# Hybrid RG-LRU and attention block on eight cores: VectorE copies the next line's first gate sums out of PSUM while ScalarE takes its square roots

## The reference, cut to what matters

```python
def rglru_coeffs(xc, wa, ba, wx, bx, lam):
    r = jax.nn.sigmoid(jnp.einsum('blnd,nde->blne', xb, wa) + ba)   # recurrence gate
    i = jax.nn.sigmoid(jnp.einsum('blnd,nde->blne', xb, wx) + bx)   # input gate
    log_a = -LRU_C * r * jax.nn.softplus(-lam)
    a = jnp.exp(log_a)
    coef = jnp.sqrt(-jnp.expm1(2.0 * log_a))                        # sqrt(1 - a*a)
    return a, coef * (i * xf)
# then h[t] = a[t] * h[t-1] + b[t] per channel, forward and backward, both added,
# times gelu(gate branch), then the output projection
```

## Time and profile before

| what | value |
| --- | --- |
| median of 3 timed runs (lowest, highest) | 3960.41 us (3803.53, 4261.93) |
| the profiled execution's own time | 3797.51 us |
| its span, first to last instruction, slowest core (core 2) | 3795.9 us |
| spans of the 8 cores | 3766.0 to 3795.9 us |
| mean granted TensorE clock of the cores | 0.957 to 0.962 of full speed |

### The profile page before, as it was taken

How to read it: one execution, slowest core, us unless ns; L and a number is a source line. 1 busy time by engine, 2 the same in 40 slices (tenths; PEclk the granted TensorE clock), 3 DMA queues, 4 the chain that set the end, 5 groups by cost and what they waited for, 6 DMA issues and landing times.

```text
span 3795.9 us, 51533 instructions; the slowest of 8 cores (3766.0 to 3795.9 us)
## 1 busy us (share of the span) xinstructions
PE 3480.0 (92%) x15292; PEld 1460.8 (38%) x15292; DVE 2856.2 (75%) x3064; ACT 2195.1 (58%) x2549; POOL 710.0 (19%) x621
## 2 busy tenths in 40 slices
PE   5787898899899789899999999999999999999989
PEld 2333343333333223334434434434434444444434
DVE  1687786566677788898798798798798798788732
ACT  2566668677688666565465465465465465556410
POOL 2466650000000000220120120130040040040030
PEclk8899999988989799999999999999999999999999
DMA  8555657977767642322632532543543443452454
GB/s 198 150 151 154 179 165 160 205 172 169 201 157 183 169 148 71 91 89 88 164 114 88 161 115 88 154 121 92 139 134 94 126 147 93 117 161 84 119 172 139
DMA packets 282622, 523.93 MB, mean 138 GB/s; under 512 B 29968, under 2 KB 139024, under 8 KB 281104
## 3 DMA queue, kind: packets, MB, share of 16 engines
q1 hardware_dynamic: 239712, 427.82, 38.3%
q0 software_dynamic: 19312, 57.03, 9.0%
q10 hardware_dynamic: 23328, 35.79, 2.7%
HBM read 470.19 MB, written 114.56 MB: 154 GB/s over the span
## 4 chain that ended last, share of the span: by engine, by line
PE 71%; ACT 7%; DVE 7%; issue 6%; DMA 5%; SPq 2%; POOL 1%; ACTq 0%; DVEq 0%; POOLq 0%
PE psq L468 71%; SPq L452 2%; DVE acc L474 2%; ACT tmp L459 1%; DVE xt L474 1%; ACT pt L459 1%; ACT L459 1%; DMA rb<-RD 1%; DVE tq L482 1%; DMA Q<-qo 1%; ACT ab L459 1%; DMA wm<-w_mod 1%; DVE xo L482 1%; DMA x<-XC 1%; DMA wmd<-w_mod 1%
## 5 line engine op out<-in xcount | busy, mean ns | idle before, releaser
L459 ACT ACTIVATE pt<-psq 128x1024 bf16<-128x1024 f32 x1088 | 1103.0, 1022 | 881.8 <-PE psq L468 824.8
L474 DVE TENSOR_TENSOR acc<-acc,pt 128x1024 f32<-128x1024 f32 x960 | 1230.0, 1281 | 231.2 <-ACT pt L459 192.8
L468 PE MATMUL psq<-mt,wr 128*128 128x512 bf16 x3328 | 819.2, 380 | 16.7 <-ACT mt L459 8.4
L468 PE MATMUL psq<-pt,Vt 128*128 128x512 bf16 x2176 | 655.7, 380 | 41.1 <-ACT pt L459 40.7
L468 PE MATMUL psq<-qh,KT 128*128 128x512 bf16 x2176 | 651.6, 380 | 0.0
L468 PEld LDWEIGHTS psq<-mt,wr 128*128 128x128 bf16 x3328 | 321.4, 98 | 432.9 <-issue 66.4
L468 PE MATMUL psq<-hL,wt 128*128 128x512 bf16 x1664 | 413.8, 401 | 21.3 <-ACT to L459 13.4
L468 PE MATMUL psq<-aT,wr 128*128 128x512 bf16 x1408 | 333.4, 379 | 0.3 <-DVE den L474 0.3
L452 POOL DMA_DIRECT2D RD<-rec x8 | 4.3, 538 | 1721.1 <-DVE rec L486 1721.1
L468 PEld LDWEIGHTS psq<-pt,Vt 128*128 128x128 bf16 x2176 | 197.1, 97 | 332.5 <-issue 135.3
L468 PE MATMUL psq<-xc,gw 128*128 128x512 bf16 (+1 forms) x832 | 276.0, 421 | 44.9 <-ACT ab L459 39.6
(11 more groups left out here) (128 smaller groups left out, 3860.1 us busy)
## 6 DMA issues: line engine op xcount, KB each, us to landing
wr<-WFI SPq DMA_DIRECT2D x176, 512.0 KB, 3.6
wr<-WFO SPq DMA_DIRECT2D x128, 352.0 KB, 3.1
x<-XC SPq DMA_DIRECT2D x70, 512.0 KB, 8.6
xc<-XCB SPq DMA_DIRECT2D x126, 256.0 KB, 6.6
wr<-WOL SPq DMA_DIRECT2D x64, 320.0 KB, 4.7
XC<-xo SPq DMA_DIRECT2D x80, 228.0 KB, 3.2
xt<-xT SPq DMA_DIRECT2D x8, 2048.0 KB, 12.1
wmd<-w_mod SPq DMA_DIRECT2D x16, 1024.0 KB, 6.1
```

The costliest lines, as they stand in the source:

```text
L459: return S.add("act", lambda e: e.activation(out=out, in_=in_, func=func, **kw), reads, writes, dur=0.17 + 0.000833 * fsz(out) + 0.09 * na ...
L468: return S.add("pe", lambda e: e.matmul(out, lhsT=lhsT, rhs=rhs, start=start, stop=stop), reads, writes, dur=d, lat=0.3)
L474: return S.add(eng, lambda e: e.tensor_tensor(out=out, in0=in0, in1=in1, op=op), reads, writes, dur=edur(eng, fsz(out), 1.13e-3))
```

## The change

Three things change, all in the loop over the steps.

1. At the end of a line (`idx == 4`), after the gates of step `k + 2` (the next line's first chunk of 1024), `step_copy(k + 2)` has VectorE copy both gate sums from PSUM into the `ab` and `wb` buffers that the chunk will use. The loads and the gates of step `k + 3` are emitted right behind, ahead of `window(li)`. At `idx == 0` the tanh of that chunk then reads and writes these SBUF buffers, and `gate_mm` isn't emitted again. This happens at 19 of the 20 line ends.
2. The square of the chunk at `idx == 2` moves from VectorE to ScalarE, in all 20 lines. It is emitted at `idx == 4`.
3. The planner's estimate for a VectorE copy of 1024 columns becomes 1.23 us (it was 0.82).

```diff
-                     dur=0.1 + fsz(out) * (1.1e-3 if eng == "pool" else 0.7e-3))
+                     dur=0.1 + fsz(out) * (1.1e-3 if eng == "pool" or fsz(out) == 1024 else 0.7e-3))
...
+    def step_a(k, copied=False):
...
+        if copied:
+            ab, wb = aslots[(li, c)], wslots[(li, c)]
+            sa, sx, ra, rx = ab.t[:, 0:n], wb.t[:, 0:n], [ab.r], [wb.r]
+        else:
+            ab, wb = step_slots(k)
+            sa, sx = ps2[0][:, 0:n], ps2[1][:, 0:n]
...
+    def step_copy(k):
+        ab, wb = step_slots(k)
+        cast("dve", ab.t[:, :], ps2[0][:, :], [ps[0].r, ps[1].r], [ab.r])
+        cast("dve", wb.t[:, :], ps2[1][:, :], [ps[2].r, ps[3].r], [wb.r])
...
-        if idx in (2, 3):
+        if idx == 2:
             square(k - 1, "dve")
...
             square(k - 4, "act")
+            square(k - 2, "act")
             square(k - 1, "act")
             square(k, "act")
...
             g_evict()
+            if k + 2 < nst:
+                step_copy(k + 2)
+                step_load(k + 3)
+                gate_mm(k + 3)
             window(li)
             gw_load(li + 2)
         else:
-            step_a(k + 1)
-            if k + 2 < nst:
+            step_a(k + 1, idx == 0 and k > 0)
+            if k + 2 < nst and (idx > 0 or k == 0):
                 gate_mm(k + 2)
```

More of the change, by code:

```diff
@@ L990, in flush_ev, with step_slots @@
             evq.pop(0)()
-    def step_a(k):
+    def step_slots(k):
         li, m, d, c = steps[k]
-        c0, n = chunks[c]
-        ci = d * 10 + m
         ab = acR.next() if c == 0 else aR.next()
@@ L999, in step_a @@
         wslots[(li, c)] = wb
-        nb = (n + 511) // 512
-        ra = [ps[h].r for h in range(nb)]
-        rx = [ps[2 + h].r for h in range(nb)]
-        act(ab.t[:, 0:n], ps2[0][:, 0:n], AF.Tanh, reads=ra + [lc.r], writes=[ab.r], scale=0.5, bias=lc.t[:, 40 + ci:41 + ci])
-        act(wb.t[:, 0:n], ps2[1][:, 0:n], AF.Tanh, reads=rx + [lc.r], writes=[wb.r], scale=0.5, bias=lc.t[:, 60 + ci:61 + ci])
+        return ab, wb
+    def step_a(k, copied=False):
+        li, m, d, c = steps[k]
+        c0, n = chunks[c]
+        ci = d * 10 + m
+        nb = (n + 511) // 512
+        if copied:
[4 more added lines that the diff above has]
+            sa, sx = ps2[0][:, 0:n], ps2[1][:, 0:n]
+            ra = [ps[h].r for h in range(nb)]
+            rx = [ps[2 + h].r for h in range(nb)]
+        act(ab.t[:, 0:n], sa, AF.Tanh, reads=ra + [lc.r], writes=[ab.r], scale=0.5, bias=lc.t[:, 40 + ci:41 + ci])
+        act(wb.t[:, 0:n], sx, AF.Tanh, reads=rx + [lc.r], writes=[wb.r], scale=0.5, bias=lc.t[:, 60 + ci:61 + ci])
+    def step_copy(k):
+        ab, wb = step_slots(k)
+        cast("dve", ab.t[:, :], ps2[0][:, :], [ps[0].r, ps[1].r], [ab.r])
+        cast("dve", wb.t[:, :], ps2[1][:, :], [ps[2].r, ps[3].r], [wb.r])
     def step_b(k):
```

## The result

The changed kernel is 0.57% faster: the ratio to the kernel before is 0.9943, 95% interval 0.9919 to 0.9967, about 22 us. That is the same by the 2% of a verdict, and outside of no change by its interval; a second set of runs on another chip gave 0.9959 [0.9934, 0.9985]. The profiled execution took 3792.33 us (before 3797.51). Executions in which the cores of one or both dies show a lower clock are left out of all ratios; sq_only, est_old, copy_only and before_rows128 had only such ones and so have no ratio, and their profiles and that of after_rows128 are read on the four cores of the unaffected die, that of copy_only not at all.

What follows compares the result with a forecast made beforehand. TensorE, busy 92% of the span, waits in turn with ScalarE and VectorE and loses clock behind gaps. Terms -4.5 - 4.7 + 1.8 + 4.7 + 0.8 = -1.9 us from 3797.5 gave 3796 us, range 3748 to 3830, own range 3780 to 3812.

Steps and rivals of the forecast that it cites:

- the fast rival: Root stretches: the gap closes and the clock stays up, 25 us of gap and 41 of clock gained, 3738 us; chance 0.17.
- The copies: PSUM copies on VectorE: 38 at 1.22 us, 46.4 us in sum, beside the roots in most lines.
- The tanh from SBUF: ScalarE: 38 tanh read SBUF instead of PSUM, 0.02 us more each, 0.8 us, bounds -1 to 4.8.
- The loads: Step k + 3 loads on SP's queue: emitted earlier but come no earlier, counted as nothing, bound 5 us either way.
- part 4: Root stretches: gates one step earlier; in most the gap is moved, not closed, kept gains -4.5 and -4.7 us.
- the removed waits: Behind some roots: ScalarE's waits go at three stretches, -4.5 us, and six waits for second halves of gates, -4.7 us.
- The square: Square moved to ScalarE: can push nine root stretches back by up to 1.05 us each, half taken, 4.7 us.
- VectorE's relief: VectorE gives up 20 squares of 1.21 us; net with copies +1.23 us a line, 1.8 us counted on three full lines.
- VectorE in front of TensorE: Ends of the nine forward lines: copies queue behind VectorE's work, tanh and gates wait, +33 us, 3830 us; chance 0.25.

Runs made afterwards that it cites:

- sq_only: Kernel before, with only the square of the idx 2 chunk moved to ScalarE, no copies: 731 us from first to last root, no ratio.
- est_old: Changed kernel with the planner's estimate for the copies left at 0.82 us: 701 us from first to last root, no ratio.
- copy_only: Changed kernel with the idx 2 square left on VectorE: first profile disturbed, no ratio; run again on another chip 708 us, ratio 0.998 to the kernel before.
- before_rows128: Kernel before, with the 32-row gate matmuls of groups 0 to 7 made 128 rows wide by zero weights: 690 us from first to last root, no ratio.
- after_rows128: Changed kernel with all gate matmuls of groups 0 to 7 made 128 rows wide: 704 us from first to last root, ratio 0.9966 to the kernel before.
- x_first: Kernel before, with each step's float32 x load issued ahead of its bf16 input loads on SP's queue: 743 us from first to last root, ratio 1.008.
- rows128_idx2: Kernel before, with 128-row gates only in the idx 2 chunk, whose gates follow the gap behind the roots: 720 us from first to last root, ratio 1.0001.
- one_end: Kernel before, with the change made only at the end of group 8 forward (root at 737 us): 731 us from first to last root, ratio 1.001.
- rows128_b: Repeat of before_rows128 (kernel before with wide gates) on another chip: 684 us from first to last root, ratio 0.9946 to the kernel before.
- all_but_one: Changed kernel with the old code at the end of group 8 forward only: 700 us from first to last root, ratio 0.993 to the kernel before.
- x_first_rows128: Kernel before, with x loads issued first and 128-row gates in groups 0 to 7: 689 us from first to last root, ratio 0.9927.
- evict_rows128: Changed kernel with the copied chunk's tanh pair written behind its step's fills and evictions, and wide gates: 699 us from first to last root, ratio 0.9926.

## Why the prediction was wrong

The forecast was -1.9 us on an execution like the profiled one. The measured change is -22 us, -12 to -31 by its interval. That lies between the forecast and the fast rival (3738, or -59), and the interval excludes both. On the profiled execution's time it makes 3776 us, which is inside the wide range of 3748 to 3830 only because that reaches half way to the fast rival, and outside the forecast's own 3780 to 3812. That the sign was right is no merit: -1.9 is what was left of terms of up to 4.7 us, and the gain came from a term that had been put at nothing.

**Right.** The copies take 1.22 us each, as worked out from 687 + 528 ns, and lie beside the roots. The tanh from SBUF takes 1134 ns, 0.02 us more, as taken. The Trainium skill ("VectorE: DVE Perf Modes", section on the TRN2 errata) gave twice that by its fixed parts, 0.043 us; the trace says 0.023. The idle time of the stretches fell from 33 to 10 us on core 2 (7 over the cores) where 8 was said, and grew behind them by as much. The gap is moved and not closed, and the next bank comes free only with the eviction. The loads were counted as nothing; x_first, which moved one of them, gave no gain.

**The step that failed** is in part 4: "at 878.5 it has done exactly the work that it had done before at the upper clock", with its conclusion that "the clock has as much reason to fall as before". Two things were wrong in it.

First, the size of the gates. "Eight matmuls at the upper clock take about 1.7 us" is the time of wide ones (1.92 measured, in rows128_idx2). These are half narrow: 1.34 us for four, some 2.6 for eight, and 3.37 at the clock that they had the earlier trace rows. Before, the gates ended at 879.05, behind the eviction's end at 878.5; at 878.5 the kernel before had not done that work. The row stood in the prediction's own evidence and was read for its start only.

Second, what the clock does behind a moved gap. It was forecast at 0.87 to 0.91 in the recurrence and came out at 0.92, and the lost clock, counted as unchanged, fell by 22 to 28 us. I took the gap as the cause of the low clock and didn't ask which matmuls follow it. The trace of before had a case against that: 1.94 us of gap at 737, ahead of gates of 128 rows, with a clock of 1.00 behind it. In the changed kernel a gap of 2.22 us between fills is followed by a clock of 1.00; before, 1.67 us ahead of half-narrow gates were followed by 0.63. In rows128_idx2 the gap is the same 1.66 us, the gates behind it are wide, and the clock behind the stretches is 0.87 instead of 0.75. The Trainium skill ("TensorE: Matmul & The Clock Gate", section on psum-queue depth-cycling) says that frequent short idles between groups of matmuls make the clock switch between its levels and cost throughput; here they did before and hardly did after, with the same idle time in sum, so by these runs the gap alone does not decide. Nor does the width of what follows alone: at 737 in rows128_idx2 the clock fell ahead of wide gates.

**What the change gives.** In the thirteen lengths away from groups 8 and 9 it gives 8 to 15 us, by 21 to 27 us less lost clock. rows128_idx2, which regains as much clock there with faster gates and without early ones, is as short (465 us), so the early gates are not needed for a gain of that size in these lengths. In the six lengths around groups 8 and 9 it gives 7 to 13 us with little change of the clock. What the change has there is that the next chunk's gates, 20 matmuls in these groups, are done early. The changed kernel and its variants with other lists lie at 235 to 238 us in these six, and the kernel before, sq_only, one_end, x_first and rows128_idx2 at 244 to 256; but rows128_b, without early gates, has 236, so that it is the early gates is argued and not shown. The prediction had put the removed waits at 4.5 + 4.7 = 9.2 us, by counting only those that stood directly behind the roots; all of ScalarE's waits for gates fell by 31 us on core 2 (78.4 to 47.8). A wait that goes is not a gain by itself: ScalarE's idle time fell by 34 to 44 us, but with 21 us more of squares to do and a shorter recurrence it has to.

**The costs.** The square was put at 4.7 us, bounds 0 to 9.5. Alone it is 4 to 12, around the upper bound; with the copies it is no cost, and perhaps a gain of 6 to 8, within the spread. That would be VectorE's relief, which the prediction counted on three lines only.

**The rivals.** The fast rival had the clock half right: 0.925, short of the 0.93 that was to prove it, ScalarE's wait down by 39% where half was asked. It needed the gap to close, and the gap did not. VectorE in front of TensorE appears only with wide gates, where the change costs 14 to 20 us: TensorE's waits for the copies sum to 0.3 us in the changed kernel and to 7 in after_rows128.

## What to carry to other kernels

An idle gap and a low clock behind it are two things: before you price a gap, look at which instructions stand next to it and compare their own durations with the same instruction elsewhere in the trace. Write the bounding engine's time as idle, lost clock and work; if one of them shrinks, ask whether another takes it up, as idle time did in part in rows128_idx2. Then do it by place as well: sums over the whole part hid that this run had gained in thirteen lengths and lost in six. And before adding an operation to get around slow matmuls, try to make them fast: the widening of two lines took more out of the recurrence than the change, and beside it the change made the recurrence longer.

## What the runs showed of the hardware

Four matmuls of 512 columns, of 128 and 32 rows in turn, take 1.34 us where four of 128 rows take 1.03, although the narrow ones have a quarter of the rows; from start to start that is 0.32 us a matmul against 0.22. In the profile of the changed kernel TensorE stood 0.3 us or more in 9 of the 19 windows behind the root stretches of core 2 at a granted clock of 1.00. Widening the narrow half raised the mean clock of the recurrence from 0.89 to 0.95 although TensorE's idle time grew from 73 to 116 us: here the clock did not follow idle time. But behind gaps of over 1 us it was still low in 10 of 17 stretches of that kernel's core 2.

No version is clearly best: the ratios 0.993 of all_but_one, 0.9927 of x_first_rows128 and 0.9926 of evict_rows128 overlap with that of the change, although the recurrence of the kernels with wide gates and no copies is the shortest by 9 to 18 us. A part of that is given back ahead of the first root, which the four kernels with wide gates throughout that are profiled on all cores reach at 589 to 592 us, the kernel before at 581 and 583. Why, and why the slowest core's whole time doesn't show the rest, stays open.
